# The inverse transform of a long convolution on one core: the order of its first jobs, and two of them cut by channel instead of by residue

## The reference, cut to what matters

```python
def hyena_mixer(u, ...):
    L = u.shape[1]                                    # 1024 tokens
    z = short_conv(u @ w_in + b_in, conv_w, conv_b)
    x0, x1, v = jnp.split(z, 3, axis=-1)
    s = (v * x1).astype(jnp.float32)
    g = hyena_filter(L, ...)                          # (2L, 1024), divided by its sum of magnitudes
    n = 2 * L
    y = jnp.fft.irfft(jnp.fft.rfft(s, n=n, axis=1) * jnp.fft.rfft(g, n=n, axis=0)[None],
                      n=n, axis=1)[:, :L]
    y = (y + s * skip.astype(jnp.float32)).astype(u.dtype) * x0
    return y @ w_out + b_out
```

## Time and profile before

| | |
|---|---|
| time, median of 3 runs | 2446.01 us (2444.39 to 2450.88) |
| the profiled execution | 2445.98 us, its span 2444.2 us |
| busy: PE, PEld | 2360.0 us (97%), 1899.7 us (78%) |
| busy: DVE, ACT, POOL | 1107.9 us (45%), 604.0 us (25%), 657.8 us (27%) |
| product jobs of the inverse (L1426) | 18.0 us busy, 128 records |
| transpose jobs (L1432) | 8.7 us busy, 64 records |
| the phase, from the first product to the last remainder | 454.4 to 495.5 us |

### The profile page before, as it was taken

The page is one execution under the profiler, slowest core; times in us unless marked ns, Lnnn a source line. Parts: engine busy times, 40 slices in busy tenths (PEclk is TensorE's granted clock), DMA queues, the critical chain, the costliest instruction groups (busy, mean ns, idle before and its releaser), DMA issues.

```text
span 2444.2 us, 29269 instructions
## 1 busy us (share of the span) xinstructions
PE 2360.0 (97%) x11692; PEld 1899.7 (78%) x11692; DVE 1107.9 (45%) x1131; ACT 604.0 (25%) x672; POOL 657.8 (27%) x378
## 2 busy tenths in 40 slices
PE   7999999799999999999997999999999999999996
PEld 5666773478888888888886888889897877778885
DVE  6765445542662165413366837263543124500533
ACT  4333324422100001002123636262622011111011
POOL 2212211122333333323241121222222233323331
PEclk9999999999999999999998999999999999999998
DMA  4133239512221223112111212020214221112231
GB/s 155 51 122 123 85 134 369 187 43 78 95 86 52 77 80 109 43 43 70 51 61 35 104 36 69 26 77 26 77 34 181 94 78 56 56 43 69 95 121 69
DMA packets 77507, 211.51 MB, mean 87 GB/s; under 512 B 24182, under 2 KB 28088, under 8 KB 77178
## 3 DMA queue, kind: packets, MB, share of 16 engines
q1 hardware_dynamic: 64794, 172.72, 20.7%
q10 hardware_dynamic: 8288, 29.36, 3.1%
q0 software_dynamic: 4352, 8.40, 1.1%
HBM read 165.36 MB, written 40.37 MB: 84 GB/s over the span
## 4 chain that ended last, share of the span: by engine, by line
PE 75%; DVE 3%; ACT 1%; issue 0%; ACTq 0%; DVEq 0%
PE ps L1209 63%; PE ps L539 5%; DVE T L1857 1%; PE ps L1483 1%; PE ps L586 1%; PE ps L605 1%; PE ps L568 1%; PE ps L606 1%; PE ps L607 1%; PE ps L1231 0%; DVE XN L1887 0%; PE ps L1240 0%; DVE X L2181 0%; DVE H L1880 0%; PE ps L505 0%; PE ps L524 0%
## 5 line engine op out<-in xcount | busy, mean ns | idle before, releaser
L1209 PE MATMUL ps<-H,whi 128*128 128x512 f32 x4000 | 1082.3, 392 | 21.9 <-DVE H L1924 11.3
L1209 PEld LDWEIGHTS ps<-H,whi 128*128 128x128 f32 x4000 | 749.9, 188 | 198.5 <-issue 29.6
L1209 PE MATMUL ps<-H,wlo 128*128 128x512 f32 x2000 | 617.7, 390 | 0.0
L1156 POOL CAST whi<-wraw 128x1024 fp32r<-128x1024 f32 x174 | 182.5, 1049 | 1573.0 <-PE ps L1209 844.9
L1158 POOL TENSOR_TENSOR wlo<-wraw,whi 128x1024 fp32r<-128x1024 f32 x178 | 453.6, 2548 | 53.4 <-ACT whi L673 39.5
L1209 PEld LDWEIGHTS ps<-H,wlo 128*128 128x128 f32 x2000 | 376.5, 188 | 79.3
L1209 PE MATMUL ps<-A,whi 128*128 128x512 f32 x1472 | 397.8, 392 | 8.2 <-DVE A L2213 4.9
L1209 PEld LDWEIGHTS ps<-A,whi 128*128 128x128 f32 x1472 | 278.0, 189 | 68.0 <-issue 5.3
L1209 PE MATMUL ps<-A,wlo 128*128 128x512 f32 x736 | 228.1, 391 | 0.0
L1209 PEld LDWEIGHTS ps<-A,wlo 128*128 128x128 f32 x736 | 139.3, 189 | 29.3
L2097 DVE TENSOR_TENSOR T<-ps,T 128x1024 f32<-128x1024 f32 x22 | 26.9, 1224 | 155.7 <-PE ps L1209 155.7
(11 more groups left out here) (337 smaller groups left out, 2310.6 us busy)
## 6 DMA issues: line engine op xcount, KB each, us to landing
wraw<-in_panels SPq DMA_DIRECT2D x181, 512.0 KB, 3.6
mw<-in_modp SPq DMA_DIRECT2D x24, 512.0 KB, 3.5
g<-gsp SPq DMA_DIRECT2D x16, 512.0 KB, 3.7
gr<-g SPq DMA_DIRECT2D x16, 512.0 KB, 9.8
bs<-s SPq DMA_DIRECT2D x16, 512.0 KB, 9.4
YB<-yi POOLq DMA_DIRECT2D x16, 512.0 KB, 8.8
X<-in_xT SPq DMA_DIRECT2D x4, 1024.0 KB, 10.8
s<-sa SPq DMA_DIRECT2D x8, 512.0 KB, 2.7
```

What stands on the lines that cost most here:

```text
L1156: nc.gpsimd.tensor_copy(whi[:, s, :, :], wraw[:, s, :, :]).then_inc(hi_made, 1)
L1209: last = mm(p[:, c * step:(c + 1) * step], w[:, ws, k, :], operand(act, a, k, c * step, step), start=(q == 0 and w is whi and a == 0), sto ...
```

## The change

The list `INV` begins differently. The first two product jobs take 128 channels and all sixteen residues each, where they took 256 channels and eight residues each. With that, tile 0 is complete after the first job and tile 1 after the second. The transposes of tile 0 follow the second product job, where a third product job stood between. The second product job of channels 256 to 511 comes after the transposes of tile 1 instead of before. From the seventh job on the lists are the same.

```diff
-INV = [("rows", 0, 256, 8 * _m) for _m in range(2)]
-for _c in range(1, 4):
+INV = [("rows", 0, 128, 0), ("rows", 128, 128, 0), ("tile", 0), ("rows", 256, 256, 0), ("tile", 1), ("rows", 256, 256, 8)]
+for _c in range(2, 4):
     for _m in range(2):
         INV.append(("rows", 256 * _c, 256, 8 * _m))
         INV.append(("tile", 2 * _c - 2 + _m))
```

## The result

| | before | after |
|---|---|---|
| time, median | 2446.78 us (2444.39 to 2450.88, 4 runs) | 2464.11 us (2462.19 to 2465.51, 4 runs) |
| ratio to before | | 1.0069, 95% interval 1.0056 to 1.0082 |
| the profiled execution | 2445.98 us, span 2444.2 us | 2462.19 us, span 2460.4 us |

The change makes the kernel 17 us slower. It lies outside the predicted range and on the side to which the prediction gave 0.02.

The account below looks back on a forecast made before the run. It took VectorE's three operations a tile to set the inverse phase's end, while TensorE is three quarters of the whole chain. 2445.98 us less 0.87 lead plus 0.05 for the small jobs gave 2445.2 us, range 2441.5 to 2450.0.

Parts of the forecast that it names:

- job 8: Inverse-phase product job after transposes 2, forecast unmoved at 469.38 us; its copy precedes ScalarE's high part of tile 1.
- the two jobs of 128 channels: First two inverse product jobs: same columns, twice the instructions, at most 0.1 us more each at full clock; 0.05 us taken.
- Rival 4: TensorE's instructions come late while DMA engines are full: stall of some 3.3 us behind transposes 1, 2448.4 us; chance 0.05.
- The small jobs: First two inverse product jobs in the new 128-column shape: 0.05 us added, range kept 0 to 3.6 us.
- rival 3: Small jobs slower, halves in turn or weight loads exposed: 2448.7 or 2448.1 us; chance 0.14.
- The lead: How much earlier VectorE's inverse-phase stream runs: 1.7 us at first, 0.87 us from job 8 to the last remainder.
- the cut: At unmoved job 8 VectorE waits for ScalarE's high part of tile 1, reducing the lead from 1.7 to 0.87 us.
- The copies: ScalarE's copies of the new jobs, eight pieces of 128: 1.02 us or up to 2.06 us, adding 0 to the path.
- The projection: Output projection on TensorE: reached 0.87 us earlier, still waits for VectorE; its half-clock time left unchanged.
- rival 1: Whole 1.7 us lead comes through, plus 1.3 us if the projection avoids half clock: 2443.0 us; chance 0.1.
- The new hole: New VectorE wait ahead of the remainder of tile 1, given as 0.8 us and once as 0.9.
- Rivals 1 and 2: rival 1, and the rival that the lead is lost on ScalarE or to longer slow clock: 2446.0 us, chance 0.18.

Follow-up runs that it names:

- b_gap24: Kernel of before with 24 added TensorE waits (long reached) ahead of the inverse phase; 2447.38 us, ratio to before 1.0001.
- a_early: Changed kernel plus 32 waits ahead of the inverse phase, ScalarE's high part of tile 1 and skip product of tile 3 moved behind job 6's copy; 2446.92 us, ratio 0.9996.
- b_tail64: Kernel of before with 64 added TensorE waits behind the loop over the heads, ahead of the first mixing projection; 2448.13 us, ratio to before 1.0005.
- b_gap64: Kernel of before with 64 added TensorE waits in the idle time ahead of the inverse phase; 2468.41 us, ratio to before 1.0086.
- b_gap48: Kernel of before with 48 added TensorE waits ahead of the inverse phase; 2454.06 us, ratio to before 1.0022.
- b_short: Kernel of before without the backward-state products in the head outputs (64 TensorE instructions of the loop body); 2432.85 us, ratio to before 0.9942.

## Why the prediction was wrong

**The step that failed.** It is in "Up to job 8 there are as many product jobs ...; transposes 2 and everything after keep their place on TensorE". They keep their place in time, not in memory. The part on the two jobs of 128 channels counts "twice the instructions" and prices them by how fast they are issued; it never asks where the code behind them comes to lie. Rival 4, "TensorE's instructions come late", is the right resource at the wrong place: it looked for a stall in the phase itself, 3.3 us once, while the loss comes at the head of a loop nearly 1000 us later, three times, with half clock behind each: 4.3, 7.3 and 6.3 us, together the 17.9 us. Its bound of 2448.4 us had no row for a loop's turn, and the range therefore ended at 2450.0. A row for it was on the page: 53 packets of instructions for a program of 13,855 TensorE instructions by the count in the compiled program, that is 54 blocks, although the loop over the heads alone runs four times over seven of them. This says that the loop was not fetched again; how near it was to the limit of that, the page does not say. The Trainium skill ("Runtime: NRT & Kernel Launch", Instruction fetch mechanics) gives TensorE 2048 instructions, refilled in blocks of 256, and warns that a taken branch stalls where its target is not in a window of two pages. The runs agree with the size of a block. On the window the measurement decides: a loop over seven blocks ran its second to fourth trip without a fetch, one over eight was fetched in every trip. And the stall came only where a block boundary lay close behind the head; `b_gap24`, fetched again in every trip, had none.

**What held.** Against the runs, with the slow clock taken off:

- *The small jobs*: forecast 0.05 us, measured some 0.03 us. That the halves go in turn or that the loads lie open (rival 3) did not happen. The first products take 3.58 us of full-clock work where 3.6 was worked out.
- *The lead*: forecast 1.7 us at the first sum, cut to 0.87 at job 8, less 0.05. Measured 1.69 us at the first transposes and 0.84 us at the last remainder, with a hole of 0.77 us where 0.8 us was forecast. `a_early` shows that the cut is what the prediction says: with the two ScalarE operations ahead of job 8's copy the rest of the lead comes through.
- *The copies* stayed at 1.02 us with eight pieces of 128.
- In the changed kernel's own profile the lead is 1.70 us, because the clock rose 4.0 us after the first product instead of 5.8 us. This does not belong to the change: `b_tail64`, whose code is that of before up to the end of this phase and beyond, has 3.9 us.
- *The projection*, which was left as it is with a fall to half clock that "may go away": the clock falls there in six of the thirteen profiles, before and after among them, and not in the other seven, `b_tail64` among them. So the order does not decide it, and the 1.3 us of rival 1 would have been luck.
- Two slips of the prediction change nothing: 2443.0 less 1.6 us is 2441.4 and not 2441.5, and the first transposes were to start 6.5 us behind the first product (460.9 less 454.4) and not 6.4. The new hole is once given as 0.8 us and once as 0.9; the working gives 0.8.

Rivals 1 and 2 are not separated by whole runs. Without the move of the loop the change is worth less than 1 us in 2447, and "no change" would have been right.

**What stays open.** Why a packet is under way so late at the turn, and why nothing is issued for 1.2 to 1.6 us after it has ended, is not shown. That the half clock follows from the holes is read from their order in time: it stands behind all nine heads with a hole (the changed kernel, `b_gap64`, `b_gap48`) and behind none of the second to fourth heads of the other ten profiles. But a hole is not the only thing that precedes it. Ahead of the first head TensorE is idle for 1.5 us in all thirteen profiles, with no fetch hole behind it; there the clock falls to half, for 3.4 or 6.8 us, in nine and stays full in four (before, after, `b_gap24`, `b_short`). `b_tail64`, with the same code up to that point as before, is one of the nine, so the fall there does not come from the change. A fall for 6.8 us makes the first trip 3.2 us longer, which is more than the change is worth in its own phase. No run had a hole with the clock held, so the price of the holes and that of the clock are told apart only by counting.

## What to carry to other kernels

An edit that changes the number of instructions of an engine moves all of its later code, loops too. Before costing a small edit at nothing, compare the body of each loop that follows with the engine's blocks: here one of 1592 instructions ran free in seven blocks of 256, and in eight it cost nothing (`b_gap24`), 6 us (`b_gap48`), 17 us (the changed kernel) or 21 us (`b_gap64`). How soon behind its head a boundary lies decides between the first three; the last two have it at the same place and differ in the time at half clock. When a change costs time far from where it was made, read the instruction queue's packets on the page first, and test it with idle instructions ahead of the loop: it takes one run.

## What the runs showed of the hardware

- A TensorE loop over seven blocks of 16 KB is not fetched again: 53 or 54 packets for the whole program. Over eight blocks it is fetched in every trip: 80 or 81 packets, 9 more for each of three turns.
- The fetch costs nothing by itself (`b_gap24`, 80 packets, 128.3 us a trip). It costs some 2.5 us a turn where only three weight loads stand between the loop's head and the next block. The block's packet ends 0.9 to 2.1 us behind the head, and the first load behind the hole starts 1.2 to 1.6 us after that.
- Behind each of the nine holes TensorE's clock was at 1.2 GHz for 3.4 to 10.2 us, which costs more than the holes: 10.2 us of 17.9 in the changed kernel. After the same 1.5 us of idle time ahead of the first head the clock fell in nine profiles and stayed at 2.4 GHz in four.
- Two halves of the output partitions side by side run at the same pace with 128 columns a call as with 256: some 0.03 us more for the 64 added instructions of two jobs, in spite of twice the loads.
